# Band attention: values of two units in one visit of TensorE, three buffers for the transposed probabilities, two outputs side by side in one PSUM bank

## What is computed

```python
s = jnp.einsum('bnqhd,bnkhd->bnhqk', qc, kb).astype(jnp.float32) * (HEAD_DIM_B ** -0.5) + bias[None, None]
s = jnp.where(key_valid[None, :, None, None, :], s, NEG)
p = jax.nn.softmax(s, axis=-1).astype(vb.dtype)
return jnp.einsum('bnhqk,bnkhd->bnqhd', p, vb)
```

## Time and profile before

| what | value |
|---|---|
| time, median of 3 runs | 1535.95 us (1534.48 to 1536.94) |
| profiled execution, its own time | 1534.5 us |
| its span | 1532.7 us |
| granted TensorE clock, mean | 0.998 |
| PE busy, share of the span | 99% |
| DVE, ACT, POOL busy | 63%, 38%, 16% |
| stage of the band attention | about 351 to 475.5 us |

### The profile page before, as it was taken

One profiled execution on the slowest core, in us unless ns is written; L12 is line 12 of the kernel. 1 busy time (PEld: TensorE's weight loads), 2 busy tenths in 40 slices (PEclk: granted clock), 3 DMA queues, 4 the chain that ended last, 5 costly groups with the idle time before them and its releaser, 6 DMA issues.

```text
span 1532.7 us, 26653 instructions
## 1 busy us (share of the span) xinstructions
PE 1517.3 (99%) x10896; PEld 1446.3 (94%) x10896; DVE 959.1 (63%) x1348; ACT 590.0 (38%) x1017; POOL 244.0 (16%) x322
## 2 busy tenths in 40 slices
PE   8999999999999999999999999999999999999999
PEld 8999999987778999986799999999999999999999
DVE  6745777756777443446444896666665597646753
ACT  6521021136775222135422643334333443343342
POOL 1011000001100100000000054555444310010110
PEclk9999999999999999999999999999999999999999
DMA  7425111102211524022212244433354975354563
GB/s 267 154 98 174 44 40 42 59 1 92 71 37 47 183 109 144 28 68 63 97 73 85 85 157 158 151 142 132 128 187 152 337 234 183 116 180 123 183 210 107
DMA packets 64062, 189.32 MB, mean 124 GB/s; under 512 B 7888, under 2 KB 12040, under 8 KB 63808
## 3 DMA queue, kind: packets, MB, share of 16 engines
q1 hardware_dynamic: 39392, 95.30, 18.8%
q0 software_dynamic: 24560, 92.45, 16.7%
HBM read 138.58 MB, written 54.12 MB: 126 GB/s over the span
## 4 chain that ended last, share of the span: by engine, by line
PE 52%; DMA 3%; DVE 1%; ACT 0%; issue 0%; SPq 0%
PE ps L2782 20%; PE ps L2803 20%; PE ps L419 8%; DMA a<-wdn 2%; PE ps L2663 2%; PE ps L2635 2%; DMA r_raw_b<-quads_d 1%; PE ps L2645 0%; DVE B_lo L1960 0%; PE ps L472 0%; ACT B_hi L1310 0%; ACT x_scores L1273 0%; DVE Y L2138 0%; DVE neg_max L1921 0%; ACT L499 0%
## 5 line engine op out<-in xcount | busy, mean ns | idle before, releaser
L419 PE MATMUL ps<-A_hi,w_hi 128*128 128x364 f32 x768 | 172.4, 333 | 0.3 <-DVE Y L1529 0.3
L419 PE MATMUL ps<-A_hi,w_lo 128*128 128x364 f32 x768 | 169.4, 329 | 0.0
L419 PE MATMUL ps<-A_lo,w_hi 128*128 128x364 f32 x768 | 169.2, 328 | 0.0
L383 ACT ACTIVATE w_hi<-w_raw 128x1024 fp32r<-128x1024 f32 x42 | 44.2, 1058 | 290.4 <-PE ps L419 187.3
L419 PEld LDWEIGHTS ps<-A_hi,w_hi 128*128 128x128 f32 x768 | 131.6, 188 | 7.3 <-issue 6.5
L419 PEld LDWEIGHTS ps<-A_lo,w_hi 128*128 128x128 f32 x768 | 133.6, 188 | 0.0
L419 PEld LDWEIGHTS ps<-A_hi,w_lo 128*128 128x128 f32 x768 | 133.4, 188 | 0.0
L387 DVE TENSOR_TENSOR w_lo<-w_raw,w_hi 128x1024 fp32r<-128x1024 f32 x42 | 51.1, 1221 | 103.2 <-ACT w_hi L383 103.2
L2782 PE MATMUL ps<-t_hi,wq_hi 128*128 128x272 f32 x480 | 99.3, 288 | 0.3 <-issue 0.3
L2782 PE MATMUL ps<-t_lo,wq_hi 128*128 128x272 f32 x480 | 99.2, 288 | 0.0
L2782 PE MATMUL ps<-t_hi,wq_lo 128*128 128x272 f32 x480 | 99.1, 288 | 0.0
(11 more groups left out here) (316 smaller groups left out, 3554.7 us busy)
## 6 DMA issues: line engine op xcount, KB each, us to landing
w_raw<-slabs SPq DMA_DIRECT2D x67, 512.0 KB, 3.5
quads_d<-quad_sum POOLq DMA_DIRECT2D x64, 272.0 KB, 2.9
w_raw<-wdn POOLq DMA_DIRECT2D x32, 512.0 KB, 4.0
r_raw_a<-quads_d SPq DMA_DIRECT2D x56, 272.0 KB, 3.0
r_raw_b<-quads_d SPq DMA_DIRECT2D x56, 272.0 KB, 3.2
quads_d<-hid_stage POOLq DMA_DIRECT2D x48, 272.0 KB, 3.0
Y<-xT POOLq DMA_DIRECT2D x16, 546.0 KB, 4.3
y_d<-Y POOLq DMA_DIRECT2D x16, 546.0 KB, 3.2
```

The source lines that it names most:

```text
L383: e.activation(WH[:, par], RAW[:, par], ACT.Copy).then_inc(s.w_hi, 1)
L419: ins = e.matmul(PS[:, 3 * par + c, 0:CH], wt[:, wpar, w], xt[:, col:col + CH], start=(first and n == 0 and m == 0), stop=(last and n == l ...
```

## The change

TensorE visits the values only at odd steps, for two units: at step n (odd) those of n-2 and of n-1, at step 1 those of 0 alone; unit 35 stays behind the loop. The outputs of two units stand side by side in bank 7, an odd unit's in columns 128 to 255. ScalarE reads both at the odd step, after both are complete. Since a unit's probabilities now live a step longer, PT and PT5 get a third buffer, and the copies wait for the values of unit n-3.

```diff
-        PT = [at(f"pt{r}", [P, 4, 256], F32, W0 + 5120 * r) for r in range(2)]
-        PT5 = [at(f"pt5{r}", [P, 256], F32, W0 + 5120 * r + 4096) for r in range(2)]
+        PT = [at(f"pt{r}", [P, 4, 256], F32, W0 + 5120 * r) for r in range(3)]
+        PT5 = [at(f"pt5{r}", [P, 256], F32, W0 + 5120 * r + 4096) for r in range(3)]
...
             def o_out(n):
                 j, b = divmod(n, 9)
-                e.wait_ge(s.pv_done, 2 * n + 2)
+                e.wait_ge(s.pv_done, 2 * min(n + 1 + n % 2, N_U))
                 q0, c0_, w = (P * b, 0, P) if b < 8 else (SEQ, 64, 64)
+                c0_ += P * (n % 2)
...
             def pt_copy(n):
...
-                if n >= 2:
-                    e.wait_ge(s.pv_done, 2 * (n - 1))
+                if n >= 3:
+                    e.wait_ge(s.pv_done, 2 * (n - 2))
...
                 pt_copy(n)
-                if n:
+                if n % 2:
+                    if n > 1:
+                        o_out(n - 2)
                     o_out(n - 1)
                 prepare(n)
...
-                if n:
+                if n % 2:
                     e.wait_ge(s.o_used, n)
...
-                    rhs = PT[n % 2][0:w, kt] if kt < 4 else PT5[n % 2][0:w, :]
+                    rhs = PT[n % 3][0:w, kt] if kt < 4 else PT5[n % 3][0:w, :]
...
-                        ins = e.matmul(PS[rows, 7, 0:P], lhs[:, rows], rhs[:, h * P:(h + 1) * P],
+                        ins = e.matmul(PS[rows, 7, P * (n % 2):P * (n % 2) + P], lhs[:, rows], rhs[:, h * P:(h + 1) * P],
...
                     item(j, x, n)
-                if n:
+                if n % 2:
+                    if n > 1:
+                        values(n - 2)
                     values(n - 1)
                 if n + 2 < N_U:
                     scores(n + 2)
```

More of the change, by code:

```diff
@@ L547, in pt_piece @@
             if p == 2:
-                return PT5[n % 2][0:rows, 0:w]
-            return PT[n % 2][:, :, :].rearrange("p a b -> p (a b)")[0:rows, 512 * p:512 * p + w]
+                return PT5[n % 3][0:rows, 0:w]
+            return PT[n % 3][:, :, :].rearrange("p a b -> p (a b)")[0:rows, 512 * p:512 * p + w]
         ITEM_A = {1: 11, 7: 9, 8: 10}
```

## The result

The changed kernel takes 1542.76 us (median of 6 runs, 1541.49 to 1543.49), the kernel before beside it 1536.41 us (1534.48 to 1537.62). The ratio is 1.0043, 95% interval 1.0033 to 1.0053: slower by 6.35 us, where 6.5 was forecast.

The account below looks back on a forecast made before the run. TensorE was taken to bound the kernel and the band attention. New waits of 9.2 us less 2.7 us of saved switches gave +6.5 us, so 1542.4 us against 1535.95, range 1537.8 to 1546.8.

Parts of the forecast that it names:

- Fewer visits: Band attention on TensorE: values visits fall from 36 to 19, saving 17 shape switches of 0.17 us, 2.7 us gained.
- the walk: Step-by-step reckoning of all 36 band-attention steps in the new order from durations read in the trace; change +6.5 us.
- What the missing visit hid: Band attention: TensorE newly waits for biased scores (6.3 us) and probability copies (3.1 us), less 0.2: 9.2 us.
- Third buffer: Probability buffers: it removes a wait that no row shows; counted as nothing.
- Outputs in pairs: ScalarE's paired output copies at odd steps: their delay stays hidden; uncovered, up to 1 us at each of 9 steps.
- ScalarE's queue: Rival: paired copies push ScalarE's tasks behind them into the exponentials; +11 us, 1547 us, chance 0.09.
- After the stage: Behind band attention: TensorE's waits move along with the end of the values, so the whole 6.5 us reaches the end.
- Drains decide: Rival: even steps lose no more than their 0.17 us drain; -2.7 us, 1533.2 us, chance 0.08.
- no effect: Rival: the change does not act, since waits merely shift; 1536 us within noise, chance 0.08.
- Only the scores' wait: Rival: transposes at odd steps find their chain done, only scores wait; +3.4 us, 1539.3 us, chance 0.15.

Follow-up runs that it names:

- short chain: Bias and exponentials cut to the first 128 columns: 1532.87 us on the kernel before, 1532.23 us on the changed kernel, against 1535.30 us for the kernel before uncut.
- filler: Changed kernel with the products of unit n-1 done once more at each even step, output unread: 1549.84 us against 1535.30 us for the kernel before.
- single visits: Kernel before with only the third PT buffer and two output halves, values still visited every step: 1535.44 us against 1535.30 us before, ratio 1.0001.
- copies later: Changed kernel with ScalarE's two output copies a step later, behind the copy of the probabilities: 1545.64 us against 1536.36 us for the kernel before.
- pairs behind the scores: Changed kernel with the pair of values behind the same step's scores: 1549.85 us against 1534.75 us before; with output copies a step later 1542.00 against 1536.36.
- even steps: Changed kernel with the pairs of values at even steps, units 34 and 35 behind the loop: 1541.72 us against 1534.75 us for the kernel before.

## Why the prediction was right

**Fewer visits, 2.7 us.** Right as a count: 23 gaps before the values for 38, 2.6 us less; the direct switch to the scores costs 0.17 without a wait, as the short chain shows. That the drains are a gain by themselves is shown only in part, 1.1 us in the stage of the 1.9 that the walk gave with the short chain.

**What the missing visit hid, 9.2 us.** Right, and shown in three ways: the waits stand in the trace at the forecast steps (0.63 for 0.63 at step 14, 0.30 for 0.33 at 22, 0.22 for 0.2 at 23, 0.95 for 1.05 at 17, 1.0 for 0.96 at 35); a filler of 17.0 us fits into them for 9.8; and a short chain removes the loss. The terms come out one by one: 6.2 us more before the scores, for 6.3 - 0.2; 3.0 us more before the transposes, for 3.1; 2.7 us less for the values, for 2.7. By starts of transposes the walk of the new order fell behind before by 0.42, 0.79, 1.10 at steps 4, 6, 8 in the trace, for 0.43, 0.80, 1.11 in the walk, and by 5.78 at step 34, for 5.49. (The prediction shows the walk's waits, not these running sums; from its waits the one at step 34 comes out at 5.5.) The sum was 6.5 and the stage gave 6.8. Of the 0.3 that the walk lacks nearly all is there by step 20 (3.30 for 3.03); it was not followed further.

**Third buffer, nothing.** Right: single visits, 0.0.

**Outputs in pairs, hidden.** Right for this order: copies later, no gain. The rival of ScalarE's queue is out, though it is real one order away (pairs behind the scores).

**After the stage.** Right in the main. From the last load of the values the weight loads in the profiles of both kernels keep the same distance to 0.1 us, a few single loads to 0.2, through the next 720 us. Only behind that, where the chain of the page passes over transfers of the down projection's weights, do the profiles part: the rest of the changed kernel is 2.1 us longer there than that of before, and so is that of the kernel with single visits, by 1.5, whose time is that of before. In the changed kernel 1.5 of the 2.1 gather between 1246.3 and 1249.7 us, where the granted clock is 0.50, behind a stand of TensorE of 1.95 us; the kernel with single visits has no such stretch, but a stand of 2.37 us where that of before has 0.60. So the whole delay of the stage arrives, and nothing takes it up. That the stretch belongs to the change isn't shown: 6.8 and 2.1 would be 8.9 us, and the interval of the time ends at 8.1.

**The rivals.** Drains decide and no effect: excluded by the waits and the ratio. Only the scores' wait: excluded, transposes stand 3.0 us longer (5.1 in the list of waits). ScalarE's queue: excluded for this order by the later copies.

One sentence of the forecast was wrong without harm: the products are not "53 ns each" but 109 ns, two side by side. Their sum was right, so the change's sum was.

## What to carry to other kernels

Work that keeps the bottleneck engine busy can also be the cover for a chain on the others; before it is bunched, measure the spare of each wait behind it, here 0.67 and 0.7 us under a visit of 1.25. A table of waits that shows almost none doesn't say how far the next one is; the distance between an operand's arrival and its use in the timeline does. And a gain read off one place of a trace belongs to the state in which that place was reached.

## What the runs showed of the hardware that was not expected

An fp32 entry of the trace costs some 0.85 ns per column at the granted 2.4 GHz: 109 ns for a transpose of 128 columns, 216 for an entry of a product of 256, both at full width, and 109 for a half-width one of 128. Two products on the two 64-column halves of the array start 7 ns apart and run at the same time, so that 20 of them take 1.07 us; the same result computed at full width, with half of the output thrown away, took 2.03 us. The Trainium skill, TensorEngine Tiling (Array Packing), Key Properties, states that tiles work independently and in parallel, which these two figures bear out.

In several profiled executions the granted clock fell from 2.4 to 1.2 GHz for 3.4 us in the middle of the work. In the three places that bear on this case TensorE had stood shortly before: 1.95 us until 1245.2 in the changed kernel, 0.66 and 0.86 us until 453.6 and 454.9 with even steps, 2.33 us until 476.1 with pairs behind the scores. Each cost some 1.5 us. Whether an order with more waits brings them on more often is open: the kernel with single visits stood 2.37 us among the same transfers and has no such stretch there.
